# Value projection in chunks of 512 columns by half of the contraction rows, token mixing in four PSUM banks, and the square sum of one token tile moved beside the projection of the other

## The reference

```python
h = rmsnorm(x, norm_mix_g[l])
proj = jnp.einsum('bsd,dc->bsc', h, w_in[l])
u, v, bg, cg, xs, ga, gb = jnp.split(proj, split_at, axis=-1)
u = jax.nn.gelu(u, approximate=False)
v = rmsnorm(jax.nn.gelu(v, approximate=False), norm_v_g[l])
a = spatial_gating(u, v, w_s[l], b_s[l])     # per group of 128 channels: w (128x128 tokens, masked) @ v + b, times u
c = bg * causal_dwconv(cg * xs, conv_w[l])
```

## Time and profile before

| | |
|---|---|
| median of 3 runs | 1090.09 us (1087.91 to 1091.85) |
| the profiled execution | 1089.74 us, its span 1088.0 us |
| TensorE matmul busy | 1043.0 us, 96% of the span |
| VectorE busy | 745.2 us, 68% |
| ScalarE busy | 564.0 us, 52% |
| mean granted TensorE clock | 0.986 |
| DMA | 179.23 MB, mean 165 GB/s |

### The profile page before, as it was taken

The page is one execution under the profiler, slowest core; times in us unless marked ns, Lnnn a source line. Parts: engine busy times, 40 slices in busy tenths (PEclk is TensorE's granted clock), DMA queues, the critical chain, the costliest instruction groups (busy, mean ns, idle before and its releaser), DMA issues.

```text
span 1088.0 us, 20725 instructions
## 1 busy us (share of the span) xinstructions
PE 1043.0 (96%) x8260; PEld 1014.0 (93%) x8260; DVE 745.2 (68%) x992; ACT 564.0 (52%) x780; POOL 6.6 (1%) x20
## 2 busy tenths in 40 slices
PE   7999999999999999899789999999998999999997
PEld 7999999999999999788679999999997899999997
DVE  6666655567656466877848877777865668777775
ACT  6445566555443334434646555555644665555554
POOL 0000000000000000000000000000020000000000
PEclk9999999999999999999979999999999999999999
DMA  8636654665665545334317666564322466655652
GB/s 278 203 104 206 206 200 161 195 190 177 213 193 182 202 157 194 114 97 139 117 37 215 196 193 189 175 193 141 119 57 59 155 174 182 187 174 177 193 170 78
DMA packets 201509, 179.23 MB, mean 165 GB/s; under 512 B 17444, under 2 KB 190066, under 8 KB 201458
## 3 DMA queue, kind: packets, MB, share of 16 engines
q1 hardware_dynamic: 201458, 178.51, 52.9%
HBM read 177.45 MB, written 1.05 MB: 164 GB/s over the span
## 4 chain that ended last, share of the span: by engine, by line
PE 83%; DVE 11%; ACT 3%; issue 1%; DMA 1%; SPq 0%; DVEq 0%; ACTq 0%
PE psum L580 23%; PE psum L581 23%; PE psum L582 23%; DVE whl L1520 3%; PE psum L587 3%; PE psum L588 3%; PE psum L589 3%; ACT whl L1114 1%; PE psum L878 1%; DVE stat L1894 1%; PE psum L877 1%; DMA raw<-ffn_w_up 1%; PE psum L853 1%; DVE stat L2044 1%; PE psum L862 1%
## 5 line engine op out<-in xcount | busy, mean ns | idle before, releaser
L580 PE MATMUL psum<-hT,whl 128*128 128x256 f32 x1520 | 433.0, 285 | 1.1 <-DVE hT L1595 0.6
L582 PE MATMUL psum<-hT,whl 128*128 128x256 f32 x1520 | 430.7, 283 | 0.0
L581 PE MATMUL psum<-hT,whl 128*128 128x256 f32 x1520 | 430.6, 283 | 0.0
L1520 DVE TENSOR_TENSOR whl<-raw,whl 128x2048 fp32r<-128x2048 f32 (+2 forms) x145 | 297.2, 2056 | 97.5 <-ACT whl L1114 97.1
L1114 ACT ACTIVATE whl<-raw 128x2048 fp32r<-128x2048 f32 (+2 forms) x145 | 249.0, 1718 | 115.8 <-DMA raw<-w_ff 66.4
L580 PEld LDWEIGHTS psum<-hT,whl 128*128 128x128 f32 x1520 | 292.1, 192 | 5.0 <-issue 3.3
L581 PEld LDWEIGHTS psum<-hT,whl 128*128 128x128 f32 x1520 | 292.1, 192 | 0.8
L582 PEld LDWEIGHTS psum<-hT,whl 128*128 128x128 f32 x1520 | 291.9, 192 | 0.0
L580 PE MATMUL psum<-lat,whl 128*128 128x256 f32 (+1 forms) x512 | 146.2, 286 | 5.1 <-DVE whl L1520 5.1
L582 PE MATMUL psum<-lat,whl 128*128 128x256 f32 (+1 forms) x512 | 145.4, 284 | 0.0
L581 PE MATMUL psum<-lat,whl 128*128 128x256 f32 (+1 forms) x512 | 145.3, 284 | 0.0
(11 more groups left out here) (233 smaller groups left out, 1365.6 us busy)
## 6 DMA issues: line engine op xcount, KB each, us to landing
raw<-w_ff SPq DMA_DIRECT2D x32, 1024.0 KB, 5.4
raw<-w_in SPq DMA_DIRECT2D x24, 1024.0 KB, 5.1
raw<-ffn_w_up SPq DMA_DIRECT2D x44, 512.0 KB, 5.1
q_sb<-ffn_w_up SPq DMA_DIRECT2D x44, 512.0 KB, 5.1
raw<-da_w_qkv SPq DMA_DIRECT2D x12, 1024.0 KB, 5.1
q_sb<-ffn_w_down SPq DMA_DIRECT2D x22, 512.0 KB, 3.8
raw<-ffn_w_down SPq DMA_DIRECT2D x22, 512.0 KB, 3.7
raw<-w_proj_a SPq DMA_DIRECT2D x4, 1024.0 KB, 5.5
```

Of the source, the lines that this page charges most:

```text
L580: mm(dst, weight(n, 0, cols, kt, c0, m), hi, start=start, stop=False, skip_group_check=True)
L581: mm(dst, weight(n, 0, cols, kt, c0, m), lo, start=False, stop=False, skip_group_check=True)
L582: return mm(dst, weight(n, 1, cols, kt, c0, m), hi, start=False, stop=stop, skip_group_check=True)
L1520: tt(whl[:, slot, 1, 0:w], landing(n)[:, 0:w], whl[:, slot, 0, 0:w].bitcast(F32), ALU.subtract).then_inc(lo_ready, 1)
```

## The change

It has five parts.

1. The value chunks hold half of the contraction rows (4 `kt`) by 512 columns: chunks 0 and 1 are the two halves for columns 0 to 511, chunks 2 and 3 for columns 512 to 1023. The DMA halves of a chunk are 2 `kt` each, with rows of 2 KB where they had 1 KB.
2. `v_rows` makes the projection with 512 moving columns, token tile 0 first and then token tile 1. A token tile has a PSUM bank of its own, and `v_first` says when token tile 0 of a pair of chunks is complete.
3. ScalarE takes the four banks in the order (columns low, tile 0), (low, tile 1), (high, tile 0), (high, tile 1), and makes the square sum of tile 0 before it takes the last bank.
4. `mix_tokens` uses four banks, `up[0]`, `up[1]`, `px` and `py`, and no longer waits on `mix_read`; it waits on `vec_read` instead, once. On VectorE `mix_scale` stands ahead of `take_lambda`.
5. VectorE makes the `lo` halves of chunk 1 ahead of the four copies to `xT`.

```diff
             for n in range(N_MIX):
-                dst = landing(n).rearrange("p (t c) -> p t c", c=PAIR)
-                src = w_in[:, :, IN_V + n * PAIR:IN_V + (n + 1) * PAIR]
-                sp.dma_start(dst[:, 0:KT // 2, :], src[:, 0:KT // 2, :]).then_inc(half_landed[n], 16)
-                sp.dma_start(dst[:, KT // 2:, :], src[:, KT // 2:, :]).then_inc(rest_landed[n], 16)
+                dst = landing(n).rearrange("p (t c) -> p t c", c=2 * PAIR)
+                src = w_in[:, n % 2 * (KT // 2):(n % 2 + 1) * (KT // 2), IN_V + n // 2 * 2 * PAIR:IN_V + (n // 2 + 1) * 2 * PAIR]
+                sp.dma_start(dst[:, 0:KT // 4, :], src[:, 0:KT // 4, :]).then_inc(half_landed[n], 16)
+                sp.dma_start(dst[:, KT // 4:, :], src[:, KT // 4:, :]).then_inc(rest_landed[n], 16)
...
-            def v_tile(n):
-                def first(kt):
-                    if kt == 0:
+            def flat(b):
+                return b.rearrange("p a b -> p (a b)")
+            def v_rows(n):
+                order = [(t, at) for t in range(TT) for at in range(KT // 2)]
+                for t, at in order:
+                    kt = n % 2 * (KT // 2) + at
+                    if t == 0 and at == 0:
                         pe.wait_ge(half_lo, n + 1)
-                    if kt == KT // 2:
+                    if t == 0 and at == KT // 4:
                         pe.wait_ge(lo_ready, n + 1)
-                    if n == 0:
+                    if t == 0 and n < 2:
                         pe.wait_ge(h_ready, max(2, kt + 1))
-                return first
+                    w_hi, w_lo = [weight(n, part, 2 * PAIR, at, 0, 2 * PAIR) for part in range(2)]
+                    last = tokens(flat(bank[n // 2 * 2 + t]), n, w_hi, w_lo, hi_lo(hT, kt), t, kt == 0, kt == KT - 1)
+                    if t == 0 and kt == KT - 1:
+                        last.then_inc(v_first, 1)
+                last.then_inc(chunk_used, 1)
             for c in range(4):
-                project_tokens(N_V + c, hT, first=v_tile(c))
+                v_rows(N_V + c)
...
                 pe.wait_ge(v_norm, TT)
                 pe.wait_ge(ws_read, 4)
+                pe.wait_ge(vec_read, 1)
                 for g in range(A_GROUPS):
-                    if g >= 4 and g % 2 == 0:
-                        pe.wait_ge(mix_read, g - 2)
                     for t in range(TT):
-                        last = mm(up[g // 2 % 2][:, g % 2, t * P:(t + 1) * P], vtok[:, t, g * P:(g + 1) * P],
+                        last = mm(x_bank[g // 2][:, g % 2, t * P:(t + 1) * P], vtok[:, t, g * P:(g + 1) * P],
                                   wsT[:, g, :], start=True, stop=True)
...
+            def take_v(g, t):
+                if t == 0:
+                    act.wait_ge(v_first, g + 1)
+                else:
+                    free_wait(N_V + 2 * g + 1)
+                fn(vtok[:, t, 2 * g * PAIR:2 * (g + 1) * PAIR], bank[2 * g + t][:].rearrange("p a b -> p (a b)"),
+                   ACT.Gelu).then_inc(bank_free[2 * g + t], 1)
             for c in range(4):
...
-                free_wait(n)
-                fn(vtok[:, :, c * PAIR:(c + 1) * PAIR], bank[c][:], ACT.Gelu).then_inc(bank_free[c], 1)
-            for c in range(4):
-                act.wait_ge(bank_free[c], 1)
+                if c == 1:
+                    for t in range(TT):
+                        take_v(0, t)
             for t in range(TT):
+                take_v(1, t)
+                act.wait_ge(bank_free[t], 1)
+                act.wait_ge(bank_free[2 + t], 1)
                 if t > 0:
                     act.wait_ge(v_sq, t)
                 fn(t_flat, vtok[:, t, :], ACT.Square, accum_out=vstat[:, 0, t:t + 1]).then_inc(v_sq, 1)
...
+            split_lo_half(1, 0)
+            split_lo_half(1, 1)
             for b, src in enumerate((up[0], up[1], px, py)):
                 dve.wait_ge(x_turned, b + 1)
                 copy(xT[:, 2 * b:2 * b + 2, :], src[:]).then_inc(x_read, 1)
-            split_lo_half(1, 0)
-            split_lo_half(1, 1)
...
-                ts(subln[:], gain("da_subln_g_2", 0), 1.0 - LAMBDA_INIT, None, ALU.mult)
+                ts(subln[:], gain("da_subln_g_2", 0), 1.0 - LAMBDA_INIT, None, ALU.mult).then_inc(vec_read, 1)
...
                 if spatial:
+                    mix_scale()
                     take_lambda()
-                    mix_scale()
```

More of the change, by code:

```diff
@@ L331, in build @@
         rest_landed = [sem(f"rest_landed{n}") for n in range(N_MIX)]
-        half_hi, half_lo = sem("half_hi"), sem("half_lo")
+        half_hi, half_lo, v_first = sem("half_hi"), sem("half_lo"), sem("v_first")
         mix_turned, mix_g_read = sem("mix_turned"), sem("mix_g_read")
@@ L1665, in _ @@
                 ts(vtok[:, t, :], vtok[:, t, :], vstat[:, 2, t:t + 1], None, ALU.mult).then_inc(v_norm, 1)
+            mix_bank = [up[0], up[1], px, py]
             def mix_scale():
@@ L1674, in mix_scale @@
                     stt(mixed[:, g, :].rearrange("p (t i) -> p t i", t=TT),
-                        up[g // 2 % 2][:, g % 2, :].rearrange("p (t i) -> p t i", t=TT),
+                        mix_bank[g // 2][:, g % 2, :].rearrange("p (t i) -> p t i", t=TT),
                         gain("norm_v_g", g), rows, ALU.mult, ALU.add).then_inc(mix_read, 1)
```

## The result

| | before | after |
|---|---|---|
| median of the runs | 1089.52 us (17 runs, 1087.91 to 1091.85) | 1083.12 us (17 runs, 1080.48 to 1086.79) |
| profiled execution, span | 1089.7 us, 1088.0 us | 1082.53 us, 1080.7 us |
| ratio after / before | | 0.9943, 95% interval 0.9934 to 0.9953 |

The change takes 6.4 us off the median; by the ratio that is 0.57%. Forecast were 4.0 us, to 1086.1. The direction is right, the size is too small by 2.4 us.

The account below looks back on a forecast made before the run. TensorE was taken as the bound (busy 96%, 83% of the chain). Savings of 1.27 + 0.37 + 2.35 = 4.0 us gave 1085.7 us for the profiled execution, near 1086.1 for the median; range 1083.5 to 1088.9.

Parts of the forecast that it names:

- the width: Value projection: 96 matmuls of 512 columns replace 192 of 256, saving 1.27 us.
- rival A: Value projection: the wider matmuls save nothing, at 0.24 us each, giving 1087.4 us; chance 0.07.
- rival B: Token mixing: its wait returns as a wait for `ws_read`, 2.75 us gained in all, 1087.3 us; chance 0.10.
- Rival D: Attention stages: stretches at half the granted clock may shift or grow, making the kernel slower than before; chance 0.06.
- Mixing, 2.35 us: Token mixing: with four banks TensorE's wait for VectorE goes, 3.84 us instead of 6.19, 2.35 us saved.
- Copies, 0.37 us: Value projection: TensorE's wait for the `lo` half of chunk 1 behind the copies to `xT` goes, 0.37 us saved.
- Second `lo` half of chunk 0: Projection start: third `kt` wants this half at 14.8 us, VectorE ends it near 14.3, so no loss.
- Start-up, 0.37 us: First three value matmul starts take 0.73 us instead of 0.36; this 0.37 us was kept, bounds 0 and twice that.
- Behind chunk 7: Everything after chunk 7 hangs on TensorE's own pace; each stage should stand 4.0 us earlier, with no further gain.

Follow-up runs that it names:

- copies_only: Kernel before with one edit: both `lo` halves of chunk 1 made ahead of the four copies to `xT`; 1088.17 us, ratio 0.9993.
- order0_warm7: Changed kernel with 7 matmuls of ones before the first transposes, and chunk 0 taking `kt` 0 and 1 of both token tiles first; 1082.35 us, ratio 0.9943.
- experiment 6: Changed kernel with both square sums put behind the last Gelu again; 1083.49 us, ratio 0.9938.
- late kind: Traces in which the granted clock rises near 14 us; the kernel before then takes 48.5 us from first value matmul to chunk 7.
- proj_only: Changed kernel with the token mixing of before (two banks, waits on `mix_read`, `take_lambda` first); 1086.58 us, ratio 0.9973.
- early kind: Traces in which the granted clock rises by about 8 us; the kernel before then takes 50.6 us from first value matmul to chunk 7.
- mix_only: Kernel before with only the four-bank token mixing and `mix_scale` ahead of `take_lambda`; 1085.01 us, ratio 0.9957.
- changed_again: The changed kernel unaltered, run again for a second trace and times; 1083.03 us, ratio 0.9945.
- before_a: The kernel before, unchanged, run again for one more trace; 1087.63 us.

## Why the prediction fell short

**The mechanisms held.** Against `copies_only`, which has the narrow matmuls and neither wait, `order0_warm7` saves 23.10 - 21.86 = 1.24 us by the width; 1.27 was forecast, and rival A is out. (By the figure that the Trainium skill gives in "TensorE: Matmul & The Clock Gate", section "Wait — 56ns, not 53.3ns?", about 2.5 ns a matmul beside its columns, the estimate would have been 0.24; these traces don't agree.) No wait for `wsT` stands before the mixing, so rival B is out; its cover was 0.5 us. Part 3 was rightly given nothing: experiment 6 shows that it is not needed at all. The late kind of trace gives 4.3 us to chunk 7, beside a forecast of 4.0.

**The failed step is the sum's footing: one trace was taken as the kernel's state, and the pause of the mixing was priced at its length alone.** Rival D looked for granted clock only in the attention stages; the one pause that the change removes was never asked what it does to the clock. Term by term:
- *Mixing, 2.35 us.* It is 2.70 by length in each of the eight traces with four banks: 3.49 us for 32 records, 0.109 each, where I took 0.12. And behind the pause 1.5 us more (7.72 less 6.19) go when the clock falls: in 3 of 6 traces of before, in `copies_only` (7.30 long) and in `proj_only`; in neither of the two with the pause filled, and in none of the eight with four banks. Half the executions makes 0.8 us in the mean; filling the pause gained 1.4 (0.4).
- *Copies, 0.37 us.* 0.37 in the late kind, 1.2 in the early kind, 0.8 in the mean.
- *Second `lo` half of chunk 0, priced at nothing.* It costs 0.5 us in the early kind and nothing seen in the late.
- *Start-up, 0.37 us.* It goes with an early rise, in both kernels, and is no gain of the change.

For the early kind the terms close: 1.24 + 1.21 - 0.50 + 2.70 + 1.53 = 6.2, against 50.6 - 44.4 = 6.2. For the late kind 1.24 + 0.37 + 2.70 = 4.3, against 48.5 - 44.2 = 4.3. Of the 16 traces without dummy matmuls at the start, eight are of each kind; with half of each it is 5.2 us at chunk 7.

**Behind chunk 7** I expected nothing. At the change from the feed-forward to the next stage near 896 us the kernel before waits for a split; timeline of PE, kernel before, then after:
```profile
896.04 0.60 PE L642 MATMUL psum<-ss,ones 128*128 128x256 f32 x2
897.12 0.38 PE L580 MATMUL psum<-hT,whl 128*128 128x256 f32 x1 [0.48 <-DVE whl L1520]
```
```profile
889.54 0.60 PE L643 MATMUL psum<-ss,ones 128*128 128x256 f32 x2
889.79 0.47 PE L581 MATMUL psum<-hT,whl 128*128 128x256 f32 x1
```
1.08 us to the next matmul against 0.25. In all nine traces with the projection of before it is 0.89 to 1.12 us, in all nine with the changed projection 0.24 to 0.41. With the slower restart counted in, the third matmul of the next stage comes about 0.75 us sooner. ScalarE waits there for a transfer of `ffn_w_up`, 3.9 to 4.2 us before and at most 3.1 after. It is the projection's edit that does it, since `mix_only` and `copies_only` keep the wait and `proj_only` loses it; why the transfer lands earlier against TensorE, I did not settle. With it the account is 5.2 + 0.8 = 6.0 us, beside the measured 6.2 (0.5). That the two agree rests on half of the runs being of each kind.

**What stays open.** How often the pause costs clock is known from six traces, so roughly. The attention's stretches at half clock change from execution to execution too. Windows of the kernel after, and of `changed_again`, the same place in the work:
```profile
536.80:553.90 17.10, 11.16 (x49) 10.18 (x50) 7.42 (x17) 9.19 (x24) 0.00 (x0) 0.50 0.00 1
```
```profile
538.90:542.30 3.40, 3.23 (x15) 3.04 (x16) 2.47 (x9) 2.12 (x8) 0.00 (x0) 0.50 0.00 0
...
545.70:552.50 6.80, 3.66 (x17) 3.56 (x18) 3.15 (x6) 4.46 (x9) 0.00 (x0) 0.50 0.01 2
```
What follows chunk 7 lasts 1026.4 and 1024.6 us in `before` and `before_a`, which differ in the same way (spans 1088.0 and 1085.9), so it is worth about 2 us and can account for much of the scatter. From chunk 7 to the end the six traces of the kernel before take 1026.4 us in the mean (1024.6 to 1027.4), the seven of the changed kernel and its variants with both halves 1024.5 (1021.2 to 1027.0). Of these 1.9 us the wait near 896 us explains 0.75; whether the change also shifts the odds of the half clock in attention, these runs don't tell.

The halves don't add up either. To chunk 7 `mix_only` needs 46.4 us from the first value matmul, 4.2 less than the early kind of before, and 2.7 would be saved in the late kind: 3.4 in the mean. Its five runs show 4.9 (0.5), while the same edit on top of `proj_only` gives 3.1 (0.6). The surplus in `mix_only` is not explained.

## What to carry to other kernels

A pause of the engine that bounds the kernel has two prices: its length, and the clock behind it. Before you price a pause from one trace, take several of the kernel before and see whether the matmuls behind it always run at the same pace. A cover of less than a microsecond near the program's start depends on when the clock rises; price such a wait at both ends (here 0.37 and 1.2 us).

## What the runs showed of the hardware

- A pause of 2.3 to 2.4 us in mid-stream was followed by 3.4 us at 1.2 GHz in five of eight traces that had it, and cost 1.1 to 1.5 us up to chunk 7. With dummy matmuls in the pause neither of two traces had it, and the mean times fell by 1.4 (0.4) and 1.3 (0.7) us.
- The same kernel's clock rose at about 8 us in some executions and at 14 in others, and eight transposes took 1.1 or 1.97 us accordingly.
- Matmuls of 128 columns (fp32 values, two records each) kept 0.109 us a record over 32 records; those of 256 columns 0.12 and of 512 columns 0.227 us.
